# An fp32 two-block kernel on one core: two weight chunks of the next product prepared inside the overlapped stages, first gate tiles read out ahead of chunks

## The reference, cut to what matters

```python
# first block, layer A (HGRN2): 16 heads of 128
u = rms_norm(h, g_norm) @ w_in              # q, f, i, z
fg = lb + (1 - lb) * sigmoid(f); b = cumsum(log(fg)) per chunk of 64 tokens
A = tril(q*exp(b-b_mid) @ (k*exp(b_mid-b)).T); o = A @ v + (q*exp(b)) @ S_prev
h = h + (rms_norm(o, g_out) * silu(z)) @ w_out
# layer B (forgetting attention): 16 heads of 128
k, v, F = shared keys, values and forget sums of rms_norm(h) @ w_kv
p = softmax(q @ k.T * scale + F_q - F_k, causal); h = h + ((p @ v) * silu(z)) @ w_out
# second block: Hyena and mLSTM branches, merge, FFN (not touched)
```

## Time and profile before

| | |
|---|---|
| three runs | 2826.61 us median (2825.13 to 2829.69) |
| the profiled execution | 2828.46 us, span 2826.2 us |
| PE busy | 2725.9 us, 96% of the span |
| DVE, ACT busy | 1574.6 us (56%), 1169.9 us (41%) |
| mean granted clock of PE | 0.985 of full speed |
| stage A | about 316 to 485 us |
| a_out starts | 487.4 us |
| stage B with its heads | about 862 to 1068 us |
| b_out starts | 1072.8 us |

### The profile page before, as it was taken

How to read it: one execution, slowest core, us unless ns; L and a number is a source line. 1 busy time by engine, 2 the same in 40 slices (tenths; PEclk the granted TensorE clock), 3 DMA queues, 4 the chain that set the end, 5 groups by cost and what they waited for, 6 DMA issues and landing times. The chain is left out here.

```text
span 2826.2 us, 53234 instructions
## 1 busy us (share of the span) xinstructions
PE 2725.9 (96%) x21454; PEld 2625.1 (93%) x21454; DVE 1574.6 (56%) x1884; ACT 1169.9 (41%) x1345; POOL 65.8 (2%) x59
## 2 busy tenths in 40 slices
PE   8999999999999999999999987989999999999998
PEld 8999898999988989999999984579999999999998
DVE  6445667564455655666654444556565555554443
ACT  5433465443353554433344442024444434443332
POOL 0000011010000000100000000000010000000000
PEclk9999999999999999999999998999999999999999
DMA  6555322445544324555555550025555555555553
GB/s 219 171 178 178 127 98 83 164 168 174 176 150 140 115 97 157 187 179 178 178 195 188 186 174 23 15 73 186 189 179 187 185 186 179 182 195 186 181 183 123
DMA packets 123699, 445.96 MB, mean 158 GB/s; under 512 B 13594, under 2 KB 15925, under 8 KB 123440
## 3 DMA queue, kind: packets, MB, share of 16 engines
q1 hardware_dynamic: 122208, 438.82, 46.1%
q0 software_dynamic: 1360, 5.27, 0.6%
HBM read 441.94 MB, written 2.10 MB: 157 GB/s over the span
## 5 line engine op out<-in xcount | busy, mean ns | idle before, releaser
L1636 PE MATMUL PS<-XH,hi 128*128 128x256 f32 (+1 forms) x5152 | 1463.0, 284 | 26.9 <-DVE lo L916 17.7
L1638 PE MATMUL PS<-XH,lo 128*128 128x256 f32 (+1 forms) x5152 | 1458.6, 283 | 0.0
L1637 PE MATMUL PS<-XL,hi 128*128 128x256 f32 (+1 forms) x5152 | 1458.1, 283 | 0.0
L916 DVE TENSOR_TENSOR lo<-raw,hi 128x1024 fp32r<-128x1024 f32 x728 | 897.8, 1247 | 847.0 <-ACT hi L477 835.8
L477 ACT ACTIVATE hi<-raw 128x1024 fp32r<-128x1024 f32 x728 | 762.3, 1057 | 987.9 <-PE PS L1638 961.3
L1636 PEld LDWEIGHTS PS<-XH,hi 128*128 128x128 f32 x5152 | 974.0, 189 | 30.1 <-issue 19.6
L1637 PEld LDWEIGHTS PS<-XL,hi 128*128 128x128 f32 x5152 | 974.2, 189 | 0.1
L1638 PEld LDWEIGHTS PS<-XH,lo 128*128 128x128 f32 x5152 | 973.2, 189 | 0.0
L1698 PE MATMUL PS<-XH,hi 128*128 128x256 f32 (+1 forms) x768 | 228.8, 298 | 0.1
L1700 PE MATMUL PS<-XH,lo 128*128 128x256 f32 (+1 forms) x768 | 219.6, 286 | 0.0
L1699 PE MATMUL PS<-XL,hi 128*128 128x256 f32 (+1 forms) x768 | 219.3, 286 | 0.0
(11 more groups left out here) (330 smaller groups left out, 1603.1 us busy)
## 6 DMA issues: line engine op xcount, KB each, us to landing
raw<-stream SPq DMA_DIRECT2D x828, 512.0 KB, 3.8
H<-h_in SPq DMA_DIRECT2D x4, 544.0 KB, 7.8
y_win<-windows POOLq DMA_DIRECT2D x2, 1024.0 KB, 5.5
out<-H SPq DMA_DIRECT2D x4, 512.0 KB, 3.5
dftm<-dft POOLq DMA_DIRECT2D x1, 1024.0 KB, 6.0
w<-w POOLq DMA_DIRECT2D x2, 512.0 KB, 6.6
ml_m<-mask_ml POOLq DMA_DIRECT2D x1, 512.0 KB, 4.1
a_m<-masks_a POOLq DMA_DIRECT2D x1, 272.0 KB, 5.5
```

What stands on the lines that cost most here:

```text
L916: dve.tensor_tensor(lo[s][:, :], raw[s][:, :], hi[s][:, :].bitcast(F32), ALU.subtract)\
L1636: pe.matmul(PS[:, bank, 0:n], w_hi, x_hi, start=start, stop=False)
L1637: pe.matmul(PS[:, bank, 0:n], w_hi, x_lo, start=False, stop=False)
L1638: return pe.matmul(PS[:, bank, 0:n], w_lo, x_hi, start=False, stop=stop)
```

## The change

It has five parts, and PE's instructions and their order stay the same.

- In the last head's step of both stages ACT and DVE prepare chunks 0 and 1 of the next product. `follow` gets `ready=2` and leaves them out of the first group.
- The first piece of the product's input is split before chunk 2 (`a_first`, `b_first`), and for this ACT waits only until all chunks but the last of the stage before are used, since that one reads the upper half of the k-tiles. In stage B piece 1 is split next, ahead of the copy of the last head's probabilities.
- In a_out, a_end (the variance and normalisation of the last four heads) moves from before chunk 5 to before chunk 6, and the last piece's split from before chunk 6 to before chunk 7.
- At the start of stage A a_intra(0) and the read-out of gate tiles 0 and 1 come ahead of the first four prepared chunks on DVE.
- The memsets of a_AM, a_KT and a_VT move from the start of stage A to the first read-out of a_in.

```diff
-        def follow(eng, q, chunk, before, parts, mid=lambda: None, at=2, early={}, late={}):
+        def follow(eng, q, chunk, before, parts, mid=lambda: None, at=2, early={}, late={}, ready=0):
...
-                    chunk(q, p, gg, c)
+                    if then is not before or c >= ready:
+                        chunk(q, p, gg, c)
...
@@ ACT, stage A and a_out
                     prep(q.c0 + k)
+                if i == HEADS - 1:
+                    for k in range(2):
+                        prep(prod["a_out"].c0 + k)
                 if i >= 2:
                     a_out_copy(i - 2)
...
+            def a_first():
+                act.wait_ge(chunk_used, prod["a_out"].c0 + RING - 1)
+                a_split(0)
+
             def a_last():
-                act.wait_ge(chunk_used, prod["a_out"].c0 + RING)
-                a_split(0)
                 a_out_copy(HEADS - 2)
                 a_split(1)
...
                 a_silu(3)
+                act.wait_ge(chunk_used, prod["a_out"].c0 + RING)
                 a_split(2)
...
-                   early={3: a_last, 4: a_rest, 5: a_end, 6: lambda: a_split(3)}, late=kv_late)
+                   early={2: a_first, 3: a_last, 4: a_rest, 6: a_end, 7: lambda: a_split(3)}, late=kv_late, ready=2)
@@ ACT, stage B and b_out
+                if i == HEADS - 1:
+                    for k in range(2):
+                        prep(prod["b_out"].c0 + k)
                 if i >= 1:
                     b_pt_copy(i - 1)
...
+            def b_first():
+                act.wait_ge(chunk_used, prod["b_out"].c0 + RING - 1)
+                b_split(0)
+
             def b_last():
-                act.wait_ge(chunk_used, prod["b_out"].c0 + RING)
-                b_split(0)
+                b_split(1)
                 b_pt_copy(HEADS - 1)
                 b_gate(HEADS // 2 - 1)
-                b_split(1)
...
@@ DVE, a_in and the start of stage A
+            def a_clear():
+                for s in range(2):
+                    own_last(dve.memset(a_AM[s][:, :], 0.0))
+                    own_last(dve.memset(a_KT[s][:, :], 0.0))
+                    own_last(dve.memset(a_VT[s][:, 256:384], 0.0))
+                own_wait()
+                dve.sem_inc(S("a_cleared"), 1)
...
                 if (p, gg) == (0, 0):
                     a_first_sums()
+                    a_clear()
                 scaled(q, AQ, 0)(p, gg)
...
             a_diffs(0)
+            a_intra(0)
+            for tile in A_PLAN.tiles_at(0, 0):
+                a_gate_out(tile)
             for k in A_PLAN.first_preps:
                 prep(q.c0 + k)
-            a_intra(0)
...
@@ DVE, stage A's last head and a_out
                 for k in A_PLAN.prepared[i][0]:
                     prep(q.c0 + k)
+                if i == HEADS - 1:
+                    for k in range(2):
+                        prep(prod["a_out"].c0 + k)
                 a_key_copy(i)
                 a_masked(i)
...
+            def a_first():
+                a_split(0)
+                a_gate_out(HEADS - 1)
+
             def a_last():
-                a_gate_out(HEADS - 1)
-                a_split(0)
                 a_states(HEADS - 1)
                 a_split(1)
...
@@ DVE, b_out
-            def b_last():
+            def b_first():
                 b_pair(BZ, HEADS // 2 - 1, HEADS, "b_z")
                 b_split(0)
+
+            def b_last():
+                b_split(1)
                 b_pt_copy(HEADS - 1)
                 b_product(HEADS - 2)
-                b_split(1)
```

More of the change, by code:

```diff
@@ L763, in _, with b_rest @@
                         b_gate(m)
+            def b_first():
+                act.wait_ge(chunk_used, prod["b_out"].c0 + RING - 1)
+                b_split(0)
             def b_last():
-                act.wait_ge(chunk_used, prod["b_out"].c0 + RING)
-                b_split(0)
+                b_split(1)
                 b_pt_copy(HEADS - 1)
                 b_gate(HEADS // 2 - 1)
-                b_split(1)
+            def b_rest():
+                act.wait_ge(chunk_used, prod["b_out"].c0 + RING)
+                b_split(2)
             w2_late, w2_early, w2_last = input_pieces("w2", (3, 2), MG, META, SEQ)
             follow(act, prod["b_out"], chunk, lambda: None, [(2, nothing)],
-                   early={3: b_last, 4: lambda: b_split(2), 6: lambda: b_split(3)}, late=w2_late)
+                   early={2: b_first, 3: b_last, 4: b_rest, 6: lambda: b_split(3)}, late=w2_late, ready=2)
             q = prod["w2"]
@@ L1166, in _ @@
                     a_diffs(i + 1)
-                for tile in A_PLAN.tiles_at(i, 0):
-                    a_gate_out(tile)
+                if i:
+                    for tile in A_PLAN.tiles_at(i, 0):
+                        a_gate_out(tile)
                 for k in A_PLAN.prepared[i][0]:
                     prep(q.c0 + k)
+                if i == HEADS - 1:
+                    for k in range(2):
+                        prep(prod["a_out"].c0 + k)
                 a_key_copy(i)
@@ L1194, in _ @@
             tail = follow(dve, prod["a_out"], chunk, lambda: None, [(2, residual(prod["a_out"], "kv_norm", AB, 0, T))],
-                          early={3: a_last, 4: lambda: a_split(2), 5: a_end, 6: lambda: a_split(3)}, late=kv_late)
+                          early={2: a_first, 3: a_last, 4: lambda: a_split(2), 6: a_end, 7: lambda: a_split(3)}, late=kv_late, ready=2)
             def kv_mid():
@@ L1379, in _ @@
                             [(2, residual(prod["b_out"], "norm1", MG, META, SEQ))],
-                            early={3: b_last, 4: b_rest, 6: lambda: b_split(3)}, late=w2_late)
+                            early={2: b_first, 3: b_last, 4: b_rest, 6: lambda: b_split(3)}, late=w2_late, ready=2)
             q = prod["w2"]
```

## The result

| | median of 5 runs | lowest to highest | profiled: span | mean granted clock |
|---|---|---|---|---|
| before | 2826.61 us | 2823.86 to 2829.69 | 2826.2 us | 0.985 |
| after | 2813.42 us | 2811.38 to 2813.96 | 2811.6 us | 0.988 |

The ratio of after to before is 0.9949, with a 95% interval of 0.9938 to 0.9961: faster, by 13.2 us between the medians and 14.6 us between the two traces. The forecast was 2812, in a range of 2808.5 to 2819. A stand, here as in the prediction, is a time in which PE does nothing between two matmuls.

The account below looks back on a forecast made before the run. PE is busy nearly throughout, so only its waits or half-clock time can be won. The terms, 5.8-0.1+5.0+5.9-1.7 = 14.9 us, taken off the profiled 2828.46 us and adjusted to the median, gave 2812 us, range 2808.5 to 2819.

Parts of the forecast that it names:

- Term 1: Start of stage A: head 0's scores start earlier and a_outputs(0) moves from 342.07 to 336.2; gain 5.8 us.
- Term 2: First read-out of a_in: the memsets' new place there delays DVE's next lo, nearly covered by spare time; -0.1 us.
- The cover of 2.0 us: In a_in: DVE's lo is ready 2.0 us before PE needs it, nearly covering the memsets' 2.08 us.
- Term 3: Hand-over to a_out: earlier start 2.55, clock 1.7, chunk 5's wait 2.2, less a new 1.4 wait; gain 5.0 us.
- Term 4: Hand-over to b_out: PE starts at 1069.1 instead of 1072.78, first two chunks at full clock; gain 5.9 us.
- The clock at b_out: At b_out: PE's remaining stands of 2.4 us still bring a dip of 3.4 us at half speed; -1.7 us.
- 2.4 is beyond both: At b_out: 2.4 us of stands exceeds 2.08 us, which had a dip, and 1.98 us, which had none.
- the row that keeps the clock: Middle of stage A: a stand of 1.98 us at 436.34 had no dip after it, clock 1.00 around it.
- Waits that move on: Rival: longer waits in heads 1 and 2 or before a_out's chunk 6, with dips; 2815 to 2819 us, chance 0.2.
- That the change does nothing: Rival: head 0's Exp or XH(0) end late, both products start as now; gain 0 to 5.6 us, chance 0.05.
- blocks a queue: Rival: in head 15, hi(0) of a_out waits for weights and holds up the key copy; slower, chance 0.03.

Follow-up runs that it names:

- The single kernel: The kernel before with only the edits at the start of stage A, memsets included: 2823.55 us, ratio 0.9984.
- the repeated one: The changed kernel timed and traced once more with no edit, beside the kernel before: 2813.11 us, ratio 0.9946.
- the single kernels: The kernel before with the edits of one place alone: start of stage A 2823.55 us, a_out 2822.27 us, b_out 2822.97 us.
- the kernel with all edits together: The changed kernel plus memsets at the head of DVE's queue, a_diffs(1) between the chunks, b_out's piece 0 split in head 15's step: 2810.70 us.

## Why the prediction came out right

**Term 1, start of stage A: 5.8 forecast, 6.0 found.** Its pieces hold: a_diffs(0) led the chain, the scores no longer wait, and a wait of 1.44 us before a_outputs(0) was forecast at 1.5. The wait of 1.10 us in head 1 for GpSimd's pair had been put at 1.6. What the working left out is that DVE's and GpSimd's products stretch each other, 1.03 us for 0.77 and 1.02 for 0.42; the kernel with a_diffs(1) between the chunks gets 1.5 us by avoiding it. The Trainium skill (SBUF — State Buffer, Terms) says that the two engines arbitrate for one port pair and that the loser blocks altogether; the trace agrees that they hold each other up. The single kernel gave only 4.4 us in the median; its trace has 6.8 us at half speed, in the middle of stage A and at a_out's chunk 5, that the kernel before has not.

**Term 2, memsets: -0.1 forecast, -0.4 to -0.5 found.** The cover of 2.0 us was real, but a wait of 0.28 us was left, and from start to start such a wait costs about 0.2 us more than it shows (0.5 here, 2.2 for 2.05 at chunk 5, 1.6 for 1.42 at chunk 6). The kernel with the memsets first shows the price by its absence.

**Term 3, a_out: 5.0 forecast, 5.1 found**, and each part within 0.4 us: found were 2.9 for the start against 2.55, 1.4 for the clock against 1.7, 2.2 for chunk 5 against 2.2, and 1.5 for the new wait before chunk 6 against 1.4. The kernel with a_finish(3) back shows the last two as one trade.

**Term 4, b_out: 5.9 forecast, 5.9 found** in the profiled execution, at full clock. Both halves of the edit are in it.

**The clock at b_out: -1.7 forecast, 0 in the profiled execution, -1.5 in the repeated one.** The step reasoned from the size of the stand ("2.4 is beyond both"), and this reason is not borne out. Size in this range doesn't decide: of the seven traces with these two stands five have a stretch at half speed after them and two have none, the profiled one among these. The forecast should have stated a chance here, not a value. Nor did it see that the same uncertainty stands at stands that no edit touches: the stand of 2.0 us in the middle of stage A, which I used as the row that keeps the clock, lost 2.3 us in the profiled execution.

**How much of the agreement is luck.** The edited places were forecast well, but the sum of 14.9 against 14.6 is closer than the working deserves. Against the forecast, 1.7 us came from the clock at b_out, 1.0 from the clock behind it and 0.3 from the other terms; 2.3 us were lost in the middle of stage A, 0.7 at the first matmul and 0.3 by the memsets. The sum had the three largest of these wrong or not at all, and they nearly cancel. Between the medians the gain is 13.2 us, where the forecast had 14.6.

**The rivals.** Waits that move on: 1.10 and 1.44 us at stage A and 1.42 before chunk 6 are all that was left, and no stretch at half speed followed the last. In the traces the single kernels gain at each place what the whole gains there, so nothing was given back later. That the change does nothing, or blocks a queue: no sign of either; hi(0) of a_out didn't hold up the key copy.

What stays open is what picks the stands that bring the clock down. Where in time a stand falls would fit, since its size, its neighbours and its code are the same, but no kernel here could set it, so that wasn't shown.

## What to carry to other kernels

Where a product starts behind a stage, write down for each preparing engine what stands ahead of the first operand that the product needs, and move both the work that can be done earlier and the operand itself: each half alone left a wait of its own. Price each wait that goes from start to start of the waiting instruction, and look for what is late next; here three chains worked out end to end hit within 0.4 us. Look also at what runs beside a chain: products of DVE and GpSimd side by side took 0.6 and 0.3 us longer. For TensorE's clock, give a stand of 1 to 2.5 us a chance of a stretch of 3.4 us at half speed, 1.4 to 1.6 us dear where PE is the bound and 0.6 or less where PE waits soon after, and take its size as known only when several executions have been looked at.

## What the runs showed of the hardware that I had not expected

The clock of one program differs between executions: 20.5 and 17.1 us at half speed up to 1200 us in two traces of the changed kernel, at different stands, with all waits the same. One stand of 2.0 us, in the middle of stage A, kept the clock in 4 of 14 traces, brought it down for 3.4 us in 8 and for 6.8 us in 2. The changed kernel's ten runs lie within 2.6 us (2811.38 to 2813.96), those of the kernel before within 5.8 us in five runs and 8.1 in 27. That fewer stands make less spread would fit, but isn't shown: the five runs of the kernel with all edits together, which has the fewest, spread over 4.5 us. Products of DVE and GpSimd on 128x272 in fp32 took 0.42 and 0.77 us apart and 1.02 and 1.03 us side by side.
